# Two decoder layers on one core: head steps ahead of weight splitting and of retention squares, and the last outputs regrouped

## The reference, cut to what matters

```
for l in range(2):
    h = h + 0.5 * swiglu(rmsnorm(h, g1[l]), w_gu1[l], w_down1[l])
    h = h + mixer(rmsnorm(h, gm[l]), w_in[l], ...)
    h = h + 0.5 * swiglu(rmsnorm(h, g2[l]), w_gu2[l], w_down2[l])
out = rmsnorm(h, g_final)[:, 128:]          # the 256 real tokens

mixer(u): rq, rk, rv, rg, sq, sk, sv, ga, gb = split(u @ w_in)
    o_r = retention(rotary(rq), rotary(rk), rv)          # 8 heads
    o_r = (o_r - mean) * rsqrt(var(o_r) + eps)           # per head
    y_ret = (silu(rg) * (o_r * ret_gn)) @ w_ret_proj
    z = sq @ sk.T * scale                                # 8 heads
    a = exp(log_sigmoid(z) + reverse_cumsum(log_sigmoid(-z)) )   # strictly causal
    y_sb = (a @ sv) @ w_sb_proj
    return (sigmoid(ga) * y_ret + sigmoid(gb) * y_sb) @ w_out
```

## Time and profile before

| what | value |
|---|---|
| median of 3 runs | 1289.11 us |
| the profiled execution | 1289.24 us |
| its span, first to last instruction | 1287.4 us |
| TensorE busy | 1279.5 us (99%) |
| VectorE busy | 875.7 us (68%) |
| ScalarE busy | 703.6 us (55%) |
| mean granted TensorE clock | 0.999 |
| bytes moved | 219.3 MB, 170 GB/s |

### The profile page before, as it was taken

How to read it: one execution, slowest core, us unless ns; L and a number is a source line. 1 busy time by engine, 2 the same in 40 slices (tenths; PEclk the granted TensorE clock), 3 DMA queues, 4 the chain that set the end, 5 groups by cost and what they waited for, 6 DMA issues and landing times.

```text
span 1287.4 us, 26188 instructions
## 1 busy us (share of the span) xinstructions
PE 1279.5 (99%) x10302; PEld 1274.4 (99%) x10302; DVE 875.7 (68%) x1103; ACT 703.6 (55%) x955; POOL 55.6 (4%) x48
## 2 busy tenths in 40 slices
PE   9999999999999999999999999999999999999998
PEld 8999999999999999999999999999999999999998
DVE  7766556878777776665576665568788877766653
ACT  6444446757777554444454444467678775544442
POOL 2000001000000010000010000010000000100000
PEclk9999999999999999999999999999999999999999
DMA  7655554554344555555545555545543445655552
GB/s 295 211 173 171 179 178 150 190 168 135 126 137 147 167 179 178 172 177 174 180 159 185 179 173 173 178 164 180 176 136 132 146 152 178 197 188 183 184 180 82
DMA packets 60705, 219.30 MB, mean 170 GB/s; under 512 B 6864, under 2 KB 6992, under 8 KB 60496
## 3 DMA queue, kind: packets, MB, share of 16 engines
q1 hardware_dynamic: 60192, 217.27, 50.8%
q10 hardware_dynamic: 432, 0.85, 0.2%
HBM read 217.04 MB, written 1.05 MB: 169 GB/s over the span
## 4 chain that ended last, share of the span: by engine, by line
PE 98%; DVE 1%; ACT 1%; DMA 0%; issue 0%; DVEq 0%; ACTq 0%
PE bank L1176 31%; PE bank L1178 31%; PE bank L1177 31%; PE bank L1332 1%; PE bank L1424 1%; PE bank L1321 1%; PE bank L1304 0%; PE bank L1462 0%; DMA raw<-stream 0%; PE bank L1457 0%; PE bank L1339 0%; PE bank L1131 0%; DVE w_lo L698 0%; PE bank L1322 0%; PE bank L1135 0%; PE bank L1133 0%
## 5 line engine op out<-in xcount | busy, mean ns | idle before, releaser
L698 DVE TENSOR_TENSOR w_lo<-raw,w_hi 128x1024 fp32r<-128x1024 f32 x407 | 510.6, 1261 | 262.5 <-ACT w_hi L423 257.3
L1176 PE MATMUL bank<-xh,w_hi 128*128 128x272 f32 (+1 forms) x2224 | 641.2, 288 | 0.0
L423 ACT ACTIVATE w_hi<-raw 128x1024 fp32r<-128x1024 f32 x407 | 427.8, 1057 | 381.4 <-PE bank L1178 380.4
L1178 PE MATMUL bank<-xh,w_lo 128*128 128x272 f32 (+1 forms) x2224 | 635.9, 286 | 0.0
L1177 PE MATMUL bank<-xl,w_hi 128*128 128x272 f32 (+1 forms) x2224 | 635.5, 286 | 0.0
L1177 PEld LDWEIGHTS bank<-xl,w_hi 128*128 128x128 f32 x2224 | 418.6, 188 | 0.0
L1176 PEld LDWEIGHTS bank<-xh,w_hi 128*128 128x128 f32 x2224 | 418.3, 188 | 0.0
L1178 PEld LDWEIGHTS bank<-xh,w_lo 128*128 128x128 f32 x2224 | 418.0, 188 | 0.0
L1178 PE MATMUL bank<-gh,w_lo 128*128 128x272 f32 (+1 forms) x1016 | 290.9, 286 | 0.0
L1176 PE MATMUL bank<-gh,w_hi 128*128 128x272 f32 (+1 forms) x1016 | 290.5, 286 | 0.0
L1177 PE MATMUL bank<-gl,w_hi 128*128 128x272 f32 (+1 forms) x1016 | 289.7, 285 | 0.0
(11 more groups left out here) (213 smaller groups left out, 750.2 us busy)
## 6 DMA issues: line engine op xcount, KB each, us to landing
raw<-stream SPq DMA_DIRECT2D x407, 512.0 KB, 3.3
table<-tables SPq DMA_DIRECT2D x1, 1424.0 KB, 8.7
out<-rv_gb SPq DMA_DIRECT2D x3, 256.0 KB, 2.6
gain_h<-tokens SPq DMA_DIRECT2D x2, 272.0 KB, 6.4
raw<-stream SPq DMA_DIRECT2D x2, 256.0 KB, 4.5
rv_gb<-squares SPq DMA_DIRECT2D x1, 384.0 KB, 8.2
gain_h<-tokens ACTq DMA_DIRECT2D x1, 300.0 KB, 4.3
gain_h<-tokens ACTq DMA_DIRECT2D x1, 272.0 KB, 5.2
```

The lines of the kernel that those rows point to most:

```text
L423: eng.activation(w_hi[:, slot, :], raw[:, slot, :], ACT.Copy).then_inc(hi_ready, 1)
L698: eng.tensor_tensor(w_lo[:, slot, :], raw[:, slot, :], w_hi[:, slot, :].bitcast(F32), ALU.subtract).then_inc(lo_ready, 1)
L1176: pe.matmul(out, wh, hi, start=first, stop=False)
L1178: mm = pe.matmul(out, wl, hi, start=False, stop=last)
```

## The change

ScalarE: in steps 43, 45, 47, 49 and 51 the rounding of a piece moves from the top of the step to behind Abs, Exp and Ln of heads 3 to 7. Abs, Exp and Ln of all heads move ahead of the three reads of the retention output; both are in one step only in steps 37 and 39. VectorE: in steps 43 to 53 (the odd ones) the remainder of a piece moves from the end of the step into the next step, behind `sp_lo`. `rs_lo` moves behind `sp_lo`; both are in one step only in steps 38 and 40. At the end VectorE copies banks 0 and 2 into `out_tok` before it takes up the sums of squares, and scales the copies in place after the factor is there; features 768 to 1023 of the second token half go to bank 5, which VectorE scales instead of ScalarE; and SyncE's second and third stores change places.

```diff
+LATE_HI = range(SB0 + 6, SB0 + 2 * HEADS, 2)
+LATE_LO = range(SB0 + 6, SB0 + 2 * HEADS + 1, 2)
@@ sync
             sp_.dma_start(h_out[0:P, 0:4 * P], out_tok[:, 0, 0:4 * P]).then_inc(out_stored, 16)
+            sp_.wait_ge(out_ready, 2)
+            sp_.dma_start(h_out[P:2 * P, 0:4 * P], out_tok[:, 1, 0:4 * P]).then_inc(out_stored, 16)
             sp_.wait_ge(out_halves, 1)
             sp_.dma_start(h_out[0:P, 4 * P:], out_tok[:, 0, 4 * P:]).then_inc(out_stored, 16)
-            sp_.wait_ge(out_ready, 2)
-            sp_.dma_start(h_out[P:2 * P, 0:4 * P], out_tok[:, 1, 0:4 * P]).then_inc(out_stored, 16)
@@ scalar, mixer
-                    split_hi(base + (s + RING), (FFN + s) % RING)
+                    if s not in LATE_HI:
+                        split_hi(base + (s + RING), (FFN + s) % RING)
...
                         eng.activation(gh[:, RET_C + hd, qf:T], rn[:, qf:T], ACT.Copy).then_inc(rh_ready, 1)
+                    hd = (s - SB0) // 2
+                    if (s - SB0) % 2 == 0 and 0 <= hd < HEADS:
+                        ... Abs, Exp, Ln on sa, unchanged (from below the retention reads) ...
+                        if s in LATE_HI:
+                            split_hi(base + (s + RING), (FFN + s) % RING)
                     hd = (s - RET0 - 1) // 2          # ro, rs, rs_hi follow here
@@ scalar, end
-            for i in range(2):
+            for i, c1 in enumerate((DC * P, 6 * P)):
                 eng.wait_ge(tok_r, 1)
                 eng.wait_ge(turned, 3 + i)
-                eng.activation(out_tok[:, i, 4 * P:], bank[:, 2 * i + 1, :], ACT.Copy, scale=ms[:, i:i + 1]).then_inc(out_halves, 1)
+                eng.activation(out_tok[:, i, 4 * P:c1], bank[:, 2 * i + 1, 0:c1 - 4 * P], ACT.Copy, scale=ms[:, i:i + 1]).then_inc(out_halves, 1)
             eng.wait_ge(out_halves, 2)
+            eng.wait_ge(out_ready, 3)
@@ vector, mixer
-                    hd = (s - RET0 - 2) // 2
-                    if (s - RET0) % 2 == 0 and 0 <= hd < HEADS:
-                        ... rs_lo ...
...
                         eng.tensor_tensor(sp_lo[:, qf:], sp[:, qf:], sp_hi[:, qf:].bitcast(F32), ALU.subtract).then_inc(sp_ready, 1)
+                    if s - 1 in LATE_LO:
+                        split_lo(base + (s - 1 + RING), (FFN + s - 1) % RING)
+                    hd = (s - RET0 - 2) // 2
+                    if (s - RET0) % 2 == 0 and 0 <= hd < HEADS:
+                        eng.wait_ge(rs_ready, l * 2 * HEADS + 2 * (hd + 1))
+                        eng.tensor_tensor(rs_lo[:, qf:T], rs[:, qf:T], rs_hi[:, qf:T].bitcast(F32), ALU.subtract).then_inc(rs_split, 1)
...
                     for n in [] if s == MIX - 2 else [s - 1, s] if s == MIX - 1 else [s]:
-                        split_lo(base + (n + RING), (FFN + n) % RING)
+                        if n not in LATE_LO:
+                            split_lo(base + (n + RING), (FFN + n) % RING)
@@ vector, end
+            for i in range(2):
+                eng.wait_ge(turned, 1 + i)
+                eng.tensor_copy(out_tok[:, i, 0:4 * P], bank[:, 2 * i, :]).then_inc(out_moved, 1)
             eng.wait_ge(sums_done, 1)
             eng.tensor_scalar(ms[:, 0:2], bank[:, 4, 0:2], 1.0 / DC, EPS, ALU.mult, ALU.add).then_inc(tok_ms, 1)
             eng.wait_ge(tok_rms, 1)
             eng.reciprocal(ms[:, 0:2], r[:, 0:2]).then_inc(tok_r, 1)
+            eng.wait_ge(tok_r, 1)
+            eng.wait_ge(out_moved, 2)
             for i in range(2):
-                eng.wait_ge(tok_r, 1)
-                eng.wait_ge(turned, 1 + i)
-                eng.tensor_scalar(out_tok[:, i, 0:4 * P], bank[:, 2 * i, :], ms[:, i:i + 1], None, ALU.mult).then_inc(out_ready, 1)
+                eng.tensor_scalar(out_tok[:, i, 0:4 * P], out_tok[:, i, 0:4 * P], ms[:, i:i + 1], None, ALU.mult).then_inc(out_ready, 1)
+            eng.wait_ge(turned, 4)
+            eng.tensor_scalar(out_tok[:, 1, 6 * P:], bank[:, 5, 0:2 * P], ms[:, 1:2], None, ALU.mult).then_inc(out_ready, 1)
@@ tensor, turn_rows
+                    b, k = (5, c - 6) if i and c > 5 else (2 * i + half, c % 4)
```

More of the change, by code:

```diff
@@ L276, in trunk @@
                                                      sem("out_ready"))
-        out_halves = sem("out_halves")
+        out_halves, out_moved = sem("out_halves"), sem("out_moved")
         h_new, xh_ready, x_ready = sem("h_new"), sem("xh_ready"), sem("x_ready")
@@ L563, in mixer @@
                         eng.activation(gh[:, RET_C + hd, qf:T], rn[:, qf:T], ACT.Copy).then_inc(rh_ready, 1)
+                    hd = (s - SB0) // 2
+                    if (s - SB0) % 2 == 0 and 0 <= hd < HEADS:
+                        eng.wait_ge(z_done, l * HEADS + (hd + 1))
+                        eng.activation(sa[:, qf:], bank[:, 6, qf:SCORES], ACT.Abs).then_inc(sa_step, 1)
+                        eng.wait_ge(sa_step, l * 3 * HEADS + (3 * hd + 1))
+                        eng.activation(sa[:, qf:], sa[:, qf:], ACT.Exp, scale=-1.0).then_inc(sa_step, 1)
+                        eng.wait_ge(sa_step, l * 3 * HEADS + (3 * hd + 2))
+                        eng.activation(sa[:, qf:], sa[:, qf:], ACT.Ln, bias=1.0).then_inc(sa_step, 1)
+                        if s in LATE_HI:
+                            split_hi(base + (s + RING), (FFN + s) % RING)
                     hd = (s - RET0 - 1) // 2
@@ L576, in mixer @@
                         eng.activation(rr[:, qf:T], rr[:, qf:T], ACT.Exp, scale=-0.5).then_inc(rr_ready, 1)
[L578 to L585, removed]
                     hd = (s - SB0 - 3) // 2
@@ L881, in mixer @@
                                           ALU.subtract).then_inc(ret_ready, 1)
-                    hd = (s - RET0 - 2) // 2
-                    if (s - RET0) % 2 == 0 and 0 <= hd < HEADS:
-                        eng.wait_ge(rs_ready, l * 2 * HEADS + 2 * (hd + 1))
-                        eng.tensor_tensor(rs_lo[:, qf:T], rs[:, qf:T], rs_hi[:, qf:T].bitcast(F32), ALU.subtract).then_inc(rs_split, 1)
                     if s == SB_TAIL + 1:
@@ L1296, in turn_rows @@
                 for c in range(4 * half, 4 * half + 4):
-                    mm = pe.transpose(bank[:, 2 * i + half, P * (c % 4):P * (c % 4) + P], hg[:, c, P * i:P * i + P], ident)
+                    b, k = (5, c - 6) if i and c > 5 else (2 * i + half, c % 4)
+                    mm = pe.transpose(bank[:, b, P * k:P * k + P], hg[:, c, P * i:P * i + P], ident)
                 mm.then_inc(turned, 1)
```

## The result

| | before | after |
|---|---|---|
| median of 7 runs | 1289.01 us (1288.86 to 1289.32) | 1293.2 us (1292.99 to 1293.49) |
| profiled execution, its span | 1289.24 us, 1287.4 us | 1293.22 us, 1291.4 us |
| TensorE busy | 1279.5 us | 1279.4 us |

The ratio is 1.0032, 95% interval [1.0022, 1.0042]: slower by 4.2 us. 1293.0 us was forecast.

A forecast was written before the change was run, and what follows sets the result against it. TensorE's work was taken to bound the kernel, busy 1279.5 of 1287.4 us. Terms -1.63 + 6.06 - 0.62 (head 1's subtraction) + 0.13 = +3.94 us gave 1293.0 us; own range 1291.5 to 1294.3, 8-in-10 range 1291.0 to 1294.7.

The forecast's parts named there:

- Steps 38 and 40: Sums of squares in both layers: TensorE waits for `rs_lo` behind `sp_lo`; four pauses with restarts, +6.06 us.
- The first rival: Steps 38 and 40 on VectorE: pauses stay short, kernel not slower; 1287.0 us without any pause; chance 0.11.
- the restart: TensorE after each pause: distances behind the late matmul are longer too, about 0.10 us per pause.
- Heads 3 to 7: Subtractions of heads 5 to 7 and last value matmuls, both layers: TensorE's pauses go, -1.63 us.
- The second rival: Heads 3 to 7: nothing gained, as the mask copy or `sp_lo` becomes late; +1.6 us, 1294.6 us; chance 0.06.
- that margin of 0.1 us: ScalarE's mask copy for the next head ends about 0.1 us before TensorE asks; its distance was to stay unchanged.
- the tail addition and the next remainder start about 0.4 us later: VectorE, heads 3 to 7: delay behind the moved remainder, covered by ScalarE's mask copy; costed at nothing.
- The two terms: Program's end: small instruction of the sums +0.38 us later, first scaling from SBUF 0.25 us shorter; sum +0.13 us.
- the first store: SyncE at the end: the end moves with the first store's issue, 0.1 us later; other stores costed at nothing.
- its bounds: Steps 38 and 40 net +4.8 to +6.0 us; heads 3 to 7 gain possibly zero; end -0.03 to +0.57 us.
- the bound named for it: Heads 3 to 7: if the chain's next link, ScalarE's mask copy, were late instead, the gain would be zero.
- The third rival: TensorE: a pause lowers its clock; two falls of some 4 us each add 4 us, 1297 us; chance 0.03.

The follow-up runs named there:

- The retention part alone: Kernel before with Abs, Exp, Ln ahead of the three retention reads on ScalarE and `rs_lo` behind `sp_lo` on VectorE, nothing else; 1294.57 us, ratio 1.0042.
- the end alone: Kernel before with only the changed end: two early copies, scaling in place, bank 5 on VectorE, swapped stores; 1289.25 us, ratio 1.0001.
- the run with one copy: Kernel before; at the end VectorE copies only bank 0 into `out_tok` ahead of the sums and scales it in place; 1288.86 us, ratio 0.9998.
- the halves: Kernel before with only ScalarE's reordering (Abs, Exp, Ln ahead of the reads), 1291.37 us; or only VectorE's (`rs_lo` behind `sp_lo`), 1299.3 us.
- the two experiments that missed: Kernel before with ScalarE's reordering only, 1291.37 us against 1290.8 expected; with VectorE's `rs_lo` move only, 1299.3 us against 1297.7.
- VectorE's half alone: Kernel before with only `rs_lo` moved behind `sp_lo` on VectorE, ScalarE in its old order; 1299.3 us, ratio 1.0078.
- two small ones found on the way: On the kernel before: ScalarE's `so_tail` copy moved behind the retention reads, 1288.53 us; only bank 0 copied early at the end, 1288.86 us.

## Why the prediction was right

**Steps 38 and 40 decide.** The prediction moved the chain by 0.79 us, let `rs_lo` follow `sp_lo` by 0.49 and TensorE by 0.05. In the changed kernel Abs starts 0.31 us behind line 566 (where `ro` had started), `rs_lo` 0.50 behind `sp_lo`, and TensorE 0.05 behind it. The blocks are 5.99 us longer against 6.06. The first rival (short pauses, 1287.0 us) lacked any room on ScalarE, as said. The retention part alone, at +5.42 us, shows the place. The prediction put the restart into the distances behind the late matmul; it is in the first of them alone, and its size, 0.10 us, was right.

**Heads 3 to 7** gained 1.59 us in the pauses that were costed at 1.63. The second rival, no gain for want of margin at the mask copy, was wrong as a whole, but its place was right: that margin of 0.1 us was the one that broke, once, for head 5 of layer 1. The step of mine that failed is "the tail addition and the next remainder start about 0.4 us later, while the mask copy keeps ScalarE from taking the result earlier anyway". That is so for heads 4 to 7, whose rounded output stands behind the mask copy in program order. For heads 0 to 3 it stands ahead of Exp, and then the late addition delays Exp, the mask copy and the scores. I had read ScalarE's order for one kind of head and applied it to both. The addition was also later than said: relative to head 5's scores it starts 0.60 us later than before, not 0.4. Cost 0.18 us; the run that leaves steps 43 and 45 alone doesn't have it. That run puts back a rounding and a remainder together; that it is the remainder is read from the trace.

**The end.** The two terms were +0.38 and -0.25; the trace of the end alone has +0.34 and -0.26. A scaling of 512 columns out of SBUF takes 0.49 us, on the value taken (0.50) and at the one that the Trainium skill's rule gives (VectorE: DVE Perf Modes, "Mode 2×_2P": 0.48), not the 0.62 of one result a cycle. The time follows SyncE's stores and not ScalarE's: in the run with one copy all three of SyncE's come 0.26 us earlier and ScalarE's does not, and in the run of the end alone ScalarE's comes 0.41 us later while the time grows by no more than 0.13. The prediction had the first store decide; since SyncE's third moves with the first in both runs, nothing here parts the two.

**The parts add up.** Timed alone they give +5.42, -1.46 and +0.13, in all +4.1 us; together they cost 4.2. That the forecast comes within 0.2 us is in part luck: the two terms that it did not have, +0.18 for head 5's scores and -0.13 for the start, nearly cancel in the profiled executions, and the second is chance.

**The range.** The forecast's own range, 1291.5 to 1294.3 us, is not the sum of its bounds. With the gain in heads 3 to 7 as costed they give 1292.3 to 1294.1, and with that gain at zero, the bound named for it, up to 1295.7. The measured 1293.2 lies in all of these.

**The third rival was set aside too easily.** The prediction leaned on one row, 2.3 us without work at the full level. That is no bound: in the run of the end alone the last matmul ends at 1282.38 us and the granted clock falls at 1283.03, 0.65 us on, where in the kernel before it took 2.45 us (1282.43 to 1284.88). That pauses up to 1.61 us left the clock alone is measured; that they could not lower it is not shown. The one fall between matmuls lasted 3.4 us and cost 1.5, where the rival had taken some 4 us and 2.

**What the halves taught.** Of the two experiments that missed, one missed because a wait was moved and I counted only who waits for its result, not what is queued behind it on the same engine. The other missed by the clock, which I had taken for a rival of chance 0.03 in the forecast and left out of the expectation, though the idle times there were up to 2.43 us and not 1.61.

## What to carry to other kernels

Where one engine is busy 99% of the time, look for its pauses in the distances between starts, and before a chain is moved ahead of another on a helper engine, ask for both results when the busy engine wants them. Here it wants the squares at the end of step 38, and the head's sums only 1.7 to 2 us later, in the middle of step 39; a swap puts the later wish first. A gain that is put together with a larger loss still is one: time the parts alone. Here the change's own part for heads 5 to 7 gives 1.6 us, and with two small ones found on the way, 2.5.

## What the hardware showed that I had not expected

With VectorE's half alone, TensorE's granted clock fell to half behind an idle time of 2.43 us, not in it: 1.2 us after work had begun again, and for some 3.4 us of dense matmuls, which cost 1.5 us. The idle time in step 40 of layer 1 of the same kernel was 2.43 us too, and no such slow stretch followed: the subtraction behind it took 0.67 us. Shorter idle times between matmuls, 1.80 us in that kernel and 1.61 in the changed one, left it at 2.4 GHz. Behind the last matmul of the program the clock fell after 0.65 to 3.7 us in the eleven profiled executions. So an idle time alone doesn't tell here whether the clock will fall.

A pause of TensorE costs 0.10 us more than the wait itself, whatever its length: in thirteen pauses of 0.11 to 2.6 us in the profiles of the kernel before, the changed one and VectorE's half, the distance from the late matmul to the next is 0.10 to 0.11 us longer, and the ones behind it are as before. At head 5's scores it was 0.08. The subtraction of head 1 in layer 1 entered 0.26 us late and took 0.36 longer.
